# A 2048-wide decoder layer on one core: the openings of its two gated feed-forward stages issued in another order

## The reference, cut to what matters

```
x = x + 0.5 * swiglu(rmsnorm(x, ffn1_norm), w_gate, w_up, w_down)      # x: 256 tokens x 2048, f32; D_FF = 5632
h = rmsnorm(x, mix_norm);  x = x + mixers(h @ w_in) @ w_out            # HGRN2 heads and sparse attention
x = x + cross_attention(rmsnorm(x), rmsnorm(mem))
x = x + 0.5 * swiglu(rmsnorm(x, ffn2_norm), ...)                       # the same form again
out = rmsnorm(x, final_norm)

def rmsnorm(x, w):  return x * rsqrt(mean(x*x) + 1e-6) * w
def swiglu(h, w_gate, w_up, w_down):  return (silu(h @ w_gate) * (h @ w_up)) @ w_down
```

## Time and profile before

| | |
|---|---|
| median of 3 runs | 2004.47 us |
| the profiled execution's own time | 2006.13 us |
| its span in the trace | 2004.0 us |
| PE busy | 1972.3 us, 98% |
| DVE busy | 1447.1 us, 72% |
| ACT busy | 1038.7 us, 52% |
| chain that ended last, by engine | PE 92%, ACT 3%, DVE 2%, DMA 1% |
| first stage: opening, ten loop passes | 0 to 66 us, 66 to 489 us |
| second stage: opening, ten loop passes | up to 1333 us, 1333 to 1756 us |

### The profile page before, as it was taken

One profiled execution on the slowest core, in us unless ns is written; L12 is line 12 of the kernel. 1 busy time (PEld: TensorE's weight loads), 2 busy tenths in 40 slices (PEclk: granted clock), 3 DMA queues, 4 the chain that ended last, 5 costly groups with the idle time before them and its releaser, 6 DMA issues.

```text
span 2004.0 us, 27300 instructions
## 1 busy us (share of the span) xinstructions
PE 1972.3 (98%) x10058; PEld 1625.3 (81%) x10058; DVE 1447.1 (72%) x1772; ACT 1038.7 (52%) x1287; POOL 12.2 (1%) x19
## 2 busy tenths in 40 slices
PE   9899999999999999999999999989999999999998
PEld 7788888888888888878777888868888888888886
DVE  5799989998455555766658675678999989854444
ACT  6455555555454444455555565545555555544443
POOL 0000000000000000000002000000000000000000
PEclk9999999999999999999999999999999999999999
DMA  8666666656866557655443465565656666676654
GB/s 274 180 188 196 193 209 194 204 188 206 277 195 190 191 170 216 187 184 165 137 125 110 164 204 167 168 194 185 211 186 200 191 206 200 204 245 202 196 191 147
DMA packets 160349, 382.63 MB, mean 191 GB/s; under 512 B 13456, under 2 KB 19856, under 8 KB 159888
## 3 DMA queue, kind: packets, MB, share of 16 engines
q1 hardware_dynamic: 158176, 378.70, 59.9%
q10 hardware_dynamic: 2096, 2.87, 0.4%
HBM read 377.33 MB, written 4.19 MB: 190 GB/s over the span
## 4 chain that ended last, share of the span: by engine, by line
PE 92%; ACT 3%; DVE 2%; DMA 1%; issue 1%; SPq 0%; ACTq 0%; DVEq 0%
PE psum L1736 45%; PE psum L1772 41%; PE psum L1759 2%; ACT w_hi L567 1%; DMA w_raw<-in_gu 1%; DVE w_lo L1050 1%; PE psum L2010 1%; PE psum L2053 1%; PE psum L1748 1%; ACT prob L842 0%; PE psum L2023 0%; PE psum L2108 0%; DMA w_raw<-in_w_in 0%; PE psum L2032 0%; ACT silu_gate L842 0%
## 5 line engine op out<-in xcount | busy, mean ns | idle before, releaser
L1050 DVE TENSOR_TENSOR w_lo<-w_raw,w_hi 128x1024 fp32r<-128x1024 f32 x694 | 837.9, 1221 | 429.0 <-ACT w_hi L567 426.3
L567 ACT ACTIVATE w_hi<-w_raw 128x1024 fp32r<-128x1024 f32 x694 | 724.2, 1056 | 737.1 <-PE psum L1736 446.4
L1772 PE MATMUL psum<-w_hi,xT_hi 128*128 128x512 f32 x920 | 360.8, 392 | 6.9 <-DVE taken_mark L1247 3.9
L1772 PE MATMUL psum<-w_hi,xT_lo 128*128 128x512 f32 x920 | 358.6, 390 | 0.0
L1772 PE MATMUL psum<-w_lo,xT_hi 128*128 128x512 f32 x920 | 358.3, 389 | 0.0
L1736 PE MATMUL psum<-w_hi,ffT_hi 128*128 128x512 f32 x784 | 306.3, 391 | 0.0
L1736 PE MATMUL psum<-w_hi,ffT_lo 128*128 128x512 f32 x784 | 305.2, 389 | 0.0
L1736 PE MATMUL psum<-w_lo,ffT_hi 128*128 128x512 f32 x784 | 305.0, 389 | 0.0
L1736 PE MATMUL psum<-w_hi,xT_hi 128*128 128x512 f32 (+1 forms) x544 | 213.9, 393 | 7.1 <-DVE w_lo L1050 6.1
L1736 PE MATMUL psum<-w_hi,xT_lo 128*128 128x512 f32 (+1 forms) x544 | 210.0, 386 | 0.0
L1736 PE MATMUL psum<-w_lo,xT_hi 128*128 128x512 f32 (+1 forms) x544 | 209.6, 385 | 0.0
(11 more groups left out here) (296 smaller groups left out, 1886.2 us busy)
## 6 DMA issues: line engine op xcount, KB each, us to landing
w_raw<-in_gu SPq DMA_DIRECT2D x351, 512.0 KB, 4.3
w_raw<-in_d SPq DMA_DIRECT2D x176, 512.0 KB, 4.4
w_raw<-in_w_in SPq DMA_DIRECT2D x88, 512.0 KB, 3.7
w_raw<-in_w_out SPq DMA_DIRECT2D x32, 512.0 KB, 3.8
x<-in_x SPq DMA_DIRECT2D x8, 512.0 KB, 6.9
w_raw<-in_cw SPq DMA_DIRECT2D x8, 512.0 KB, 3.9
w_raw<-in_wk SPq DMA_DIRECT2D x8, 512.0 KB, 4.0
w_raw<-in_wq SPq DMA_DIRECT2D x8, 512.0 KB, 3.7
```

Of the source, the lines that this page charges most:

```text
L567: nc.scalar.activation(w_hi[:, slot], w_raw[:, slot], ACT.Copy).then_inc(w_hi_ready, 1)
L1050: nc.vector.tensor_tensor(w_lo[:, slot], w_raw[:, slot], w_hi[:, slot].bitcast(F32), ALU.subtract)\
L1772: mm = nc.tensor.matmul(psum[:, bank, :], act_t, w, start=(first and n == 0), stop=(last and n == 2))
```

## The change

Five things are moved, and no arithmetic is left out or added:
- The token sums on DVE stand at steps 3, 4, 9 (before 4, 5, 10) in the first stage and 5, 7, 9 (before 7, 8, 10) in the second. ACT makes their hi parts one step later than the sums (before: in the same step), and DVE their lo parts two steps later than the sums (before: one).
- Of x's squares in the first stage ACT does token tile 0 alone, and DVE does token tile 1 at the same steps.
- Variance and root of the first stage stand at step 9 ahead of that step's split (before: behind it), the inverse at step 10.
- The silu of the first stage stands at step 10 (before 9); that of the second stays at step 7.
- The products stand ahead of the split of step 14 (before: of step 15).

```diff
-FORMS_AT = ((4, 5, 10), (7, 8, 10))
+FORMS_AT = ((3, 4, 9), (5, 7, 9))
...
-            def squares(src, norm, n):
-
-                for t in range(NT):
+            def squares(src, norm, n, tiles=NT):
+
+                for t in range(tiles):
...
+                        if not base_c and k == 9:
+                            root(norm)
                         split_ahead(u0, 0, k, k + SLOTS >= U_CH, True)
-                        if k in FORMS_AT[u0 > 0]:
-                            i = FORMS_AT[u0 > 0].index(k)
+                        if k - 1 in FORMS_AT[u0 > 0]:
+                            i = FORMS_AT[u0 > 0].index(k - 1)
...
-                                squares(x, N_F1, X_SQ.index(k))
-                            if k == 9:
-                                root(norm)
-                                act.wait_ge(rstd_ready, norm + 1)
-                        if k == (U_G - 1 if base_c else U_G + 1):
+                                squares(x, N_F1, X_SQ.index(k), 1)
+                        if k == (U_G - 1 if base_c else U_G + 2):
                             act.wait_ge(unit_done, u0 + U_G)
                             if base_c:
                                 act.wait_ge(h_ready, base_c)
-                                act.wait_ge(rstd_ready, norm + 1)
+                            act.wait_ge(rstd_ready, norm + 1)
...
+                if i:
+                    dve.wait_ge(s_f32_ready, NP * nth + i)
...
+                        if not base_c and k == 9:
+                            variance(norm, sq)
+                        if not base_c and k == 10:
+                            inverse(norm)
-                        if k == U_CH - 1:
+                        if k == U_CH - 2:
                             dve.wait_ge(unit_done, u0 + U_CH)
...
-                        if k - 1 in FORMS_AT[nth]:
-                            token_lo(nth, FORMS_AT[nth].index(k - 1))
+                        if k - 2 in FORMS_AT[nth]:
+                            token_lo(nth, FORMS_AT[nth].index(k - 2))
+                        if not base_c and k in X_SQ:
+                            n = X_SQ.index(k)
+                            dve.wait_ge(x_loaded[n], 16)
+                            link(nc.vector.scalar_tensor_tensor(
+                                out=hb[:, 0, :], in0=x[:, 1, n * NW:(n + 1) * NW], scalar=1.0,
+                                in1=x[:, 1, n * NW:(n + 1) * NW], op0=ALU.mult, op1=ALU.mult,
+                                accum_out=ss[:, N_F1, 1, n:n + 1]))
...
-                        if k == (5 if base_c else 9):
+                        if base_c and k == 5:
                             variance(norm, sq)
                             inverse(norm)
```

## The result

Four runs of the changed kernel took 1990.53 us in the median (1988.56 to 1991.48), four of the kernel before 2004.57: ratio 0.9927, 95% interval 0.991 to 0.9944. It is faster by 0.7%. The profiled execution took 1991.48 us, where 1989.8 was expected; its span is 1989.7 us.

The account below looks back on a forecast made before the run. PE was taken as the bound, busy 98% of the span, so only its pauses could shrink. First stage 5.96, second 7.19 and two clock falls of 1.6 sum to 16.3 us: forecast 1988.2 us, range 1986.2 to 1991.3.

Parts of the forecast that it names:

- Unit 10's pause: First stage: earlier token sums let `w_lo` of unit 10 come at 34.5 for 36.43, so PE's 2.22 us pause goes.
- Unit 15: First stage: PE starts it at 51.04 for 55.86, 4.82 us gained, with a pause of 1.0 left.
- rival 2: First stage: variance, root and silu chain longer than summed, by 2.6 (table loads) or 2.9 us (squares); about 1991; chance 0.1.
- Unit 16: First stage, from unit 15 to 16: nothing changes in `s_lo`, weight sums and split.
- Products: First stage, ahead of unit 17: products no longer have unit 18's split before them, one spacing, 1.14 us, less.
- Second stage: Second opening: PE never pauses, unit 17 starts at 1325.98 for 1333.17, 7.19 us, with 0.9 to spare at the mark.
- The clock: Behind unit 17 in both stages: PE's fall to 1.2 GHz goes, 1.6 us each; less trust in the first stage.
- Rival 1: Clock still falls in the first stage, or in one of them: 1.6 us less gain, 1989.8 us; chance 0.2.
- Body of the loop: Loop behind the openings: PE busy 42.00 of 42 us a pass; later split of unit 18 costed at nothing.
- rival 3: Loop becomes bound by DVE, PE pauses in each of 20 passes; at 1 us a pass 2008.2 us; chance 0.03.
- Rival 4: Change does little because another wait holds the same units: within 0.2%, near 2004 us; chance 0.03.
- The sum: Whole kernel: 5.96, 7.19, 1.6 and 1.6 make 16.3 us; profiled execution 2006.13 would become 1989.8.

Follow-up runs that it names:

- experiment 3: Kernel before with only the products moved, ahead of the split of step 14: 2001.34 us, ratio 0.9979 to the kernel before.
- experiment 2: Changed kernel with the token sums and their hi and lo parts back at the old steps: 2000.93 us, ratio 0.9979 to the kernel before.
- experiment 1: Kernel before with only the token sums and their hi and lo parts at the changed steps: 1991.03 us, ratio 0.9922 to the kernel before.
- experiment 4: Changed kernel with the products back ahead of the split of step 15: 1990.33 us, ratio 0.9924 to the kernel before.
- experiment 5: Changed kernel with the first stage's variance, root, inverse and silu as before: 1988.24 us, ratio 0.991 to the kernel before.
- experiment 8: Changed kernel with first-stage variance, root and inverse behind step 9's split and silu at step 11: 1984.43 us, ratio 0.9895 to the kernel before.
- experiment 6: Changed kernel with the first stage's silu one step later, at step 11: 1986.39 us, ratio 0.9901 to the kernel before.

## Why the prediction was right, and where it was not

- **Unit 10's pause, gone as expected.** The `w_lo` of units 10, 11 and 12 end at 34.70, 37.17 and 39.05, where the prediction had 34.5, 37.0 and 38.9. (The spacing of 1.14 us used for `w_lo` isn't what the quoted 2.60 gives, which is 1.26; the rows of the changed kernel, 42.61 to 43.76 say, do show 1.14 to 1.15.)
- **Unit 15, 4.82 expected, 4.64 measured.** The chain of variance, table load, root, two splits, third sums, silu ran as written: root's load at 40.13 (expected about 40.0), third sums' end 45.6 (45.6), `w_hi` of unit 15 at 48.76 (48.59). The difference is that silu's table load began at 46.30, behind the end of `s_hi` and not 0.54 after its start. The price in rival 2 didn't come: the squares cost 0.73 to 0.82 (0.78 taken), and no load was paid twice.
- **Unit 16, nothing expected, 0.42 measured.** From unit 15 to 16 PE takes 4.30 us, for 4.72. "Nothing changes" overlooked 0.51 us for which DVE stood idle inside the weight sums of before (57.44, on its own difference). That idle time stands in the kernel before and in experiment 3 and in no other run, experiment 2 with the sums at their old steps included, so moving the sums isn't what removed it. The trace doesn't tell what it was. With unit 15: 5.06.
- **Products, 1.14 expected, 1.13 measured** in the first stage; three kernels agree on 1.13 or 1.14.
- **Second stage, 7.19 expected, 7.20 measured.** No pause was left, and unit 17 starts at 1320.59 for 1333.17; 5.38 of this were gained by 1278.95. The mark was ready at 1319.43, 1.1 us ahead (0.9 expected). Here the landing of the loads and `x_save` bounded nothing.
- **The clock, 1.6 each, measured 1.63 and 1.73** (from unit 17 to the second pass: 30.69 less 29.06, and 30.65 less 28.92). The size is right for these two profiles. The reason given for the first stage, a last pause of 0.8 in place of 1.96, isn't sufficient: 1.96 us brought a fall in the kernel before and in experiment 1, and none in experiment 4. Rival 1 was a matter of the execution, not only of the pause. The prediction also passes over a third fall, behind the 2.22 us ahead of unit 10 (granted clock 0.69 from 39 to 42 us in the kernel before). It cost nothing at the end: in experiment 3 the clock held there, and PE then paused 1.13 us ahead of unit 14, where before it had no pause.
- **Body of the loop, nothing expected, nothing measured.** Second to tenth passes keep their 42.4 us (89.24 to 131.62 and on); rival 3 has no row. Rival 4 neither, though experiments 2 and 3 show that without the sums' steps it would have been near (0.2%).
- **The sum, 16.3 expected, 14.3 measured between the spans.** The openings brought 7.82 and 8.93, 16.75 in all. What failed is the step "what an opening saves is thus kept to the end": it took the middle of the kernel as fixed, and that lost 2.8 in this profile and nothing in the next. So one profile against another carries about 3 us that belong to neither kernel. The medians' difference was 14.0 in the first comparison and 15.2 in the later one. Without the clock the openings bring 13.4 (6.19 and 7.20), so in the medians 0.6 to 1.8 us are left for the two falls, counted at 3.2, and the middle together. The kernel before shows why a fall can't be counted in full: on one chip its runs went from 2002.89 us at a granted clock of 0.999 to 2008.43 at 0.996. How the shortfall divides between clock and middle isn't shown. That the range holds the result is partly luck: its upper end was set for rivals 1 and 2, and a loss that the prediction didn't name took that room.
- What wasn't asked in the prediction: whether each moved part pays. Putting variance, root and silu back gives 1.5 us, silu behind unit 15's split 2.4 to 2.9, and both together 4.4 net of the first profile (45.64 less 41.24).

## What to carry to other kernels

An in-order engine that makes something small for another should get its input a step before its turn: moving DVE's sums one split ahead of ACT's use was worth 11 to 15 us of some 15, and nothing in arithmetic changed. Sum each part of a bundle against the one late chain; here the move of variance, root and silu lengthened it and hid behind the gain of the sums, and the squares' move did nothing. Where a table load stands behind a wait, put the wait on the instruction that uses the table, so that the load runs in the waiting time; experiments 5 and 8 show the load running there, together with another order of root and split.

## What the hardware showed

- *The clock fell and held behind the same pauses.* It fell to 1.2 GHz behind 1.96 us (before and experiment 1, unit 17), 2.22 (before, unit 10) and 2.23 (experiment 6, unit 1). It held behind 1.96 (experiment 4, unit 17), 2.17 (experiment 3, unit 10), and 2.27 and 2.92 (experiment 2, units 10 and 15). In the middle it fell behind 1.31 and 2.09 us (changed kernel) and held behind 1.27 and 2.09 (experiment 6); it fell behind 0.70 and 1.54 (experiment 5) and held behind 0.36 and 1.88 (before). Each fall cost 1.6 us. What decides stays open; no kernel here isolates it.
- *Table loads.* A load takes 1.28 us, and where nothing else is waited for, the ACTIVATE that uses the table starts within 0.02 us of its end in the profiles. The Trainium skill, page "ScalarE: Activation LUTs", section "What ACT_TABLE_LOAD costs", adds about 1.38 us of drain to each switch of set. The runs don't show it, nor where the load stands behind a wait (40.13 above).
- *Pauses without a cause in the trace.* Around 1065 us, ahead of and within some hundred matmuls of 16 columns (L2120), PE pauses 1.3 to 3.4 us in sum, another amount in most profiles, the two of the changed kernel among them. In eight of the profiles, one 0.02 MB transfer of the DMA queue that the profile calls `q8 instruction` begins 2.2 to 2.5 us before the second pause ends. The loading of PE's instructions is thus the nearest suspect; it wasn't tried.
